# A routed-expert stage of a diffusion backbone: overflow tests nested, block closed without GpSimd's drain, overflow experts on fewer buffers, filter loads issued behind the overflow weights

## The reference

```python
def moe_ffn(xt, rg_w, rg_b, re_w, re_b, w13, w2):
    g_prob = softmax(xt @ rg_w + rg_b)            # 4 groups, the best one is taken
    e_logits = xt @ re_w + re_b                   # 8 experts of that group
    e_w, e_idx = top_k(softmax(e_logits), 2)      # 2 experts per token, weights normalised
    ...
    def expert_block(args):
        xblk, e = args
        gate, up = jnp.split(xblk @ w13[e], 2, axis=-1)
        return (jax.nn.silu(gate) * up) @ w2[e]
    ...
```

## Time and profile before

| | |
|---|---|
| median of 3 runs | 2263.57 us (2260.22 to 2264.07) |
| the profiled execution | 2262.39 us, its span 2260.6 us |
| mean granted clock of TensorE | 0.962 |
| expert stage of layer 0 | about 803 to 1334 us |
| Hyena stage | about 1334 to 1722 us |
| expert stage of layer 1 | about 1723 to 2232 us |
| PE, share of the span busy | 89% |
| bytes moved by DMA | 592.09 MB |

### The profile page before, as it was taken

The page is one execution under the profiler, slowest core; times in us unless marked ns, Lnnn a source line. Parts: engine busy times, 40 slices in busy tenths (PEclk is TensorE's granted clock), DMA queues, the critical chain, the costliest instruction groups (busy, mean ns, idle before and its releaser), DMA issues. The chain is left out here.

```text
span 2260.6 us, 20875 instructions
## 1 busy us (share of the span) xinstructions
PE 2022.6 (89%) x7648; PEld 907.6 (40%) x7648; DVE 789.4 (35%) x1581; ACT 365.9 (16%) x778; POOL 238.0 (11%) x523
## 2 busy tenths in 40 slices
PE   5999999999999969997889859999996999888882
PEld 2555444444443444442333224444554444333330
DVE  3778311235333752221111124464734222111113
ACT  2111212212203121111111112110002111111111
POOL 1000000000000012221222100000000222222120
PEclk9999999999999969999999989999996999999996
DMA  9898522220103589999999961221352999999994
GB/s 363 296 368 318 206 70 87 105 102 34 65 0 114 192 343 423 421 421 422 422 422 423 416 240 59 68 84 35 122 213 99 418 423 420 422 423 422 422 413 162
DMA packets 121191, 592.09 MB, mean 262 GB/s; under 512 B 25704, under 2 KB 43872, under 8 KB 80489
## 3 DMA queue, kind: packets, MB, share of 16 engines
q1 hardware_dynamic: 94494, 548.03, 60.2%
q10 hardware_dynamic: 14412, 25.59, 3.1%
q0 software_dynamic: 12160, 16.83, 2.0%
HBM read 571.13 MB, written 42.31 MB: 271 GB/s over the span
## 5 line engine op out<-in xcount | busy, mean ns | idle before, releaser
L542 PE MATMUL bank<-w,xT 128*64 128x512 f32 x1920 | 433.1, 597 | 45.2 <-DMA w<-in_moe_w 37.3
L562 PE MATMUL bank<-w,hT 128*64 128x512 f32 x1168 | 277.4, 617 | 48.3 <-DMA w<-in_moe_w 40.7
L542 PEld LDWEIGHTS bank<-w,xT 128*64 128x64 f32 x1920 | 154.1, 138 | 310.0 <-issue 258.0
L734 DVE COPY hT<-bank 128x256 f32<-128x256 f32 x73 | 30.9, 424 | 512.9 <-PE bank L550 512.9
L1139 PE MATMUL bank<-uhi,wnh 128*128 128x512 f32 x384 | 168.4, 593 | 0.9 <-ACT uhi L888 0.9
L562 PEld LDWEIGHTS bank<-w,hT 128*64 128x64 f32 x1168 | 89.4, 141 | 185.6 <-issue 138.9
L493 ACT ACTIVATE oh<-bank 128x256 f32<-128x256 f32 x73 | 28.0, 383 | 785.0 <-PE bank L542 785.0
L1535 PE MATMUL bank<-uT,wo 128*128 128x512 f32 x256 | 133.8, 604 | 3.8 <-DVE uT L1421 3.8
L739 DVE TENSOR_TENSOR ohs<-bank,g2h 128x512 f32<-128x512 f32 x73 | 50.5, 691 | 234.6 <-PE bank L562 234.6
L1139 PEld LDWEIGHTS bank<-uhi,wnh 128*128 128x128 f32 x384 | 71.8, 190 | 86.9 <-issue 85.8
L542 PE MATMUL bank<-w13x,xT 128*64 128x512 f32 x416 | 94.4, 593 | 8.0 <-DMA w13x<-in_moe_w 8.0
(11 more groups left out here) (436 smaller groups left out, 2133.1 us busy)
## 6 DMA issues: line engine op xcount, KB each, us to landing
w<-in_moe_w SPq DMA_DIRECT2D x177, 2048.0 KB, 34.7
adab<-in_ada_w SPq DMA_DIRECT2D x24, 2048.0 KB, 11.5
w13x<-in_moe_w SPq DMA_DIRECT2D x18, 2048.0 KB, 34.1
wnh<-in_h_in_w SPq DMA_DIRECT2D x12, 1024.0 KB, 5.2
wo<-in_m_in_w SPq DMA_DIRECT2D x4, 2048.0 KB, 17.9
wo<-in_m_in_w ACTq DMA_DIRECT2D x4, 2048.0 KB, 17.6
ow<-in_m_out_w SPq DMA_DIRECT2D x8, 1024.0 KB, 6.8
d_xm<-xmb ACTq DMA_DIRECT2D x16, 385.5 KB, 5.9
```

What stands on the lines that cost most here:

```text
L542: ins = t_.matmul(b[n * C:(n + 1) * C, :].rearrange("c (g f) -> c g f", g=2), xT[:, k, half * C:(half + 1) * C], w13s[i][:, k, n], start=( ...
L562: ins = t_.matmul(b_y[m * C:(m + 1) * C, :], hT[:, k, half * C:(half + 1) * C], w2[:, u, kk, m * 512:(m + 1) * 512], start=(kk == 0), stop ...
```

## The change

Four edits, all in the expert stage.

1. The 16 overflow bodies no longer stand in 4 groups of 4 behind two levels of tests. Body o stands inside the tests of all bodies before it, so that the first test that fails jumps to the end of all.
2. The block is made with `no_gpsimd_drain=True`, by which GpSimd has no drain at the block's end.
3. The overflow steps use four of the `w13` buffers (1 to 4) and two of the `w2` slots (0 and 1), with new functions for buffer, count and previous user. Buffer 5, buffer 0 and slot 2 are left alone by them. The first overflow step's `w13` halves have buffers 1 and 2 and wait for the same products as before; its `w2` goes to slot 0 instead of slot 2.
4. SP doesn't wait for the overflow body's product2 any more. The loads of `fle` and `dfe` become a function, called where they stood. They wait for the same products as before.

```diff
--- before.py
+++ after.py
@@ -320,7 +320,7 @@
                 w13b = [w13[:, i] for i in RING] + [w13x[:]]
                 w13s = [w.rearrange("p k (g n f) -> p k n g f", g=2, n=2) for w in w13b]
                 y_half = d_y[l].rearrange("s (h d) -> (s h) d", h=2)
-                blk = c.enter_context(nc.Block())
+                blk = c.enter_context(nc.Block(no_gpsimd_drain=True))
 
                 def steps(eng, main, drain, extra):
 
@@ -330,11 +330,10 @@
                             eng.wait_ge(S["meta"], 1)
                             more = eng.value_load(meta[0:1, 0:1], min_val=0, max_val=NOV)
                     drain()
-                    for q in range(0, NOV, 4):
-                        with eng.If(more > q):
-                            for o in range(q, q + 4):
-                                with eng.If(more > o):
-                                    extra(NS + o)
+                    with ExitStack() as taken:
+                        for o in range(NOV):
+                            taken.enter_context(eng.If(more > o))
+                            extra(NS + o)
 
                 def turn(n):
 
@@ -342,7 +341,30 @@
 
                 def half_turn(p, h):
 
+                    if p >= NE:
+                        i = 1 + (2 * (p - NE) + h) % 4
+                        return i, 16 * (len(range(i, 2 * NE, NH)) + (p - NE) // 2 + 1)
                     return (2 * p + h) % NH, 16 * ((2 * p + h) // NH) + 16
+
+                def half_before(p, h):
+
+                    if p >= NE + 2:
+                        return p - 2, h
+                    last = range(half_turn(p, h)[0], 2 * NE, NH)[-1] if p >= NE else 2 * p + h - NH
+                    return last // 2, last % 2
+
+                def down_turn(p):
+
+                    if p >= NE:
+                        u = (p - NE) % 2
+                        return u, 16 * (len(range(u, NE, NB)) + (p - NE) // 2 + 1)
+                    return p % NB, 16 * (p // NB) + 16
+
+                def down_before(p):
+
+                    if p >= NE + 2:
+                        return p - 2
+                    return range(down_turn(p)[0], NE, NB)[-1] if p >= NE else p - NB
 
                 @blk.sync
                 def _(sp):
@@ -362,13 +384,13 @@
                         for h in range(2):
                             i, n = half_turn(p, h)
                             if n > 16:
-                                q, hq = (2 * p + h - NH) // 2, (2 * p + h - NH) % 2
+                                q, hq = half_before(p, h)
                                 sp.wait_ge(S["up" if hq else "upa"], LAST[q] + 1)
                             sp.dma_start(w13b[i], w13v[:, bass.ds(e, 1), h].rearrange("p o k n -> p (o k) n")).then_inc(s_w13l[i], 16)
 
                     def load_second(p, e):
-                        u, _n = turn(p)
-                        sp.wait_ge(S["yp"], LAST[p - NB] + 1)
+                        u, _n = down_turn(p)
+                        sp.wait_ge(S["yp"], LAST[down_before(p)] + 1)
                         sp.dma_start(w2[:, u].rearrange("p (h k) n -> p h k n", h=2), w2v[:, bass.ds(e, 1)].rearrange("p o h k n -> p (o h) k n")).then_inc(s_w2l[u], 16)
 
                     def main(s):
@@ -383,19 +405,21 @@
                         e = expert(1 + P + s - NS)
                         load_first(p, e)
                         load_second(p, e)
-                        sp.wait_ge(S["yp"], s + 1)
 
                     sp.wait_ge(S["meta"], 1)
                     sp.wait_ge(S["vst"], 16 * TL)
+
+                    def load_filters():
+                        if l == 0:
+                            sp.wait_ge(S["yp"], LAST[range(2, NE, NB)[-1]] + 1)
+                            for h in range(2):
+                                sp.dma_start(fle[:, :, h * 512:(h + 1) * 512], d_fl[h]).then_inc(s_fle, 16)
+                            last = range(5, 2 * NE, NH)[-1]
+                            sp.wait_ge(S["up" if last % 2 else "upa"], LAST[last // 2] + 1)
+                            sp.dma_start(dfe[:], I["dft"].rearrange("(t p) f -> p t f", p=P)).then_inc(s_dfe, 16)
+
                     steps(sp, main, lambda: None, extra)
-                    if l == 0:
-                        last = max(p for p in range(NE) if p % NB == 2)
-                        sp.wait_ge(S["yp"], LAST[last] + 1)
-                        for h in range(2):
-                            sp.dma_start(fle[:, :, h * 512:(h + 1) * 512], d_fl[h]).then_inc(s_fle, 16)
-                        last, h = max((i // 2, i % 2) for i in range(2 * NE) if i % NH == 5)
-                        sp.wait_ge(S["up" if h else "upa"], LAST[last] + 1)
-                        sp.dma_start(dfe[:], I["dft"].rearrange("(t p) f -> p t f", p=P)).then_inc(s_dfe, 16)
+                    load_filters()
                     if l == 0:
                         load_route_tables(sp, 1)
 
@@ -551,7 +575,7 @@
                         ins.then_inc(S["hps"], 1)
 
                     def product2(n):
-                        u, loads = turn(ORDER[n - 1])
+                        u, loads = down_turn(ORDER[n - 1])
                         pe.wait_ge(s_w2l[u], loads)
                         pe.wait_ge(S["hT"], n)
                         at_least(pe, S["ya"], n - 1)
```

## The result

| | before | changed |
|---|---|---|
| median of 4 runs | 2261.89 us | 2242.57 us |
| lowest to highest | 2259.92 to 2264.07 | 2240.28 to 2245.6 |
| profiled execution, its span | 2262.39, 2260.6 | 2244.76, 2243.0 |

The ratio is 0.9917, with a 95% interval of 0.9904 to 0.9929.

The account below looks back on a forecast made before the run. Weight transfers on the 16 DMA engines bound the expert stages, so only stage ends could gain. Gains of 3.2 (layer 0) and 2.3 us (layer 1), rounded down to 5.2, from 2263.57 gave 2258.4; range 2250 to 2265.5.

Parts of the forecast that it names:

- it costs 6.2 to 6.36 there: Both expert stage ends: GpSimd's removed block drain moves to L122, serial behind the barrier, costing 6.2 to 6.36 us.
- this case: Both stage ends: the drain is really gone, L122's stays at 0.12; 17.8 us less, 2245.8; chance 0.11.
- Nesting: PE's tests at both stage ends: one price per far jump, 3.6 to 5.1 us; layer 1 arrival 12.3 us earlier.
- Rival 4: PE's tests: one jump over sixteen bodies costs as much as four over four; 9.5 us slower, 2273.1; chance 0.04.
- GpSimd last at both ends: L268, both expert stages: GpSimd arrives last, at 1324.0 us in layer 0 and 2223.4 in layer 1.
- The last scatter's flight: Layer 0's end: with filter loads issued earlier, the last scatter lands 4.1 us after issue instead of 6.5.
- The jump of GpSimd: Layer 0's end: GpSimd's single jump over fifteen overflow bodies after the scatter's landing, taken as 0.5 us.
- rival 3: Layer 0: GpSimd's long jump needs a fetch, 2.8 us, and the scatter gains nothing; 0.8 less, 2262.8; chance 0.18.
- The late w2: Overflow step, layer 0: w2 is issued 15.2 us later but was waiting in line, so cost 0.
- Rival 2: Overflow step, layer 0: the later w2 is exposed and delays product2 by 15.1 us; 9.9 slower, 2273.5; chance 0.05.
- The early loads: SP, layer 0's end: filter and table loads issue from 1295 instead of 1318.46 us; alone worth nothing.
- The sum: Both stage ends: gains of 3.2 us in layer 0 and 2.3 in layer 1, rounded down to 5.2.

Follow-up runs that it names:

- e1: Changed kernel with GpSimd's drain at the expert block's end put back; 2255.41 us, ratio 0.9978.
- e2: Kernel before with only GpSimd's block drain removed; 2260.0 us, ratio 0.9992.
- e9: Changed kernel with a plain GpSimd drain added between the block's barrier and L122's drain at every stage end; 2259.1 us, single execution.
- e10: Changed kernel with a semaphore-resetting drain, then a plain one, ending GpSimd's expert-stage stream; 2244.19 us, single execution.
- e8: Changed kernel with router table loads moved to the Hyena stage and the scatter's index prepared before the wait for the result; 2242.16 us, ratio 0.9919.
- e13: Changed kernel with only the scatter's index preparation moved ahead of its wait for the result; 2243.93 us, ratio 0.9916.
- e6: Changed kernel with SP's wait for the overflow's product2 put back, so filter and table loads issue behind it; 2249.96 us, ratio 0.9951.

## Why the prediction was wrong, step by step

1. **The failed step: "it costs 6.2 to 6.36 there", at L122.** The 6.2 was read rightly as work that a drain starts, and the price is real: e1 puts it back at full length. But "L122's is then the first after the indirect transfers" took the drains as one kind. L122's resets semaphores and does not do that work (e2, e9, e10), and L123's plain one behind it finds nothing. So 6.24 us in layer 0 and 6.07 in layer 1 went away that the forecast had kept: 12.3 of the missing 14.1. The rows at hand did not forbid it: both short drains had only been seen behind the long one, and I gave this case 0.11.
2. **Nesting**: right in its place and size. PE arrives at 2208.6, which is 2218.0 on the time axis of before (9.4 later there), instead of 2231.8 (forecast 2219.5 at the latest), and at 1320.1 in layer 0 (forecast 1319). A far jump is paid once, whatever the distance, but not always with the same price: behind the early loads it is 6.2, above the forecast's bound of 5.1, and PE had time for it. Rival 4 falls.
3. **GpSimd last at both ends**: right; 1324.0 forecast and measured, but the exact agreement is luck. The profiled execution came 1.9 us later to this end, so on the time axis of before it is 1322.1, and 1.5 of the difference is SP's issue stall, which no step had.
4. **The last scatter's flight**: forecast 4.1, measured 4.1. The jump of GpSimd: 0.5 taken, 0.6 measured. In e8 and e13 the jump costs 2.6 and 2.7, the price that rival 3 was given (2.8); that a fetch is behind it is not shown.
5. **The late w2**: cost 0, right; it landed 16.5 us after its issue. Rival 2 falls.
6. **The early loads**: "Alone this is worth nothing, POOL being later" can hold only while the long drain stands inside the block (no run had this edit alone). With that drain out of the block, moved or gone, SP with late loads is the last, and the early ones are worth 4.8 us (e6 against the changed kernel). The sum had this in it without saying so, since it let SP arrive at 1322 at the latest.

With step 1 mended the sum would have been 5.2 + 12.3 = 17.5, and with SP's 1.5 us 19.0, against 19.3 measured. The other 1.7 us by which the forecast was too high lie in its base: 2263.57 from three runs, where four give 2261.89.

## What to carry to other kernels

At a barrier, list every engine's arrival and the next two behind the last: here GpSimd's drain, PE's tests and SP's loads lay over each other, and two edits that alone gave 1.8 and 5.0 us at the two ends gave 14.9 together. Of a step that is removed, ask whether what stands behind it is the same kind of instruction before moving its price there, and give that question the weight that it deserves when the two answers are 12 us apart. When a far jump follows the event that everybody waits for, its stall is on the path (layer 0 of e13, 2.7 us); in front of the event it is free (layer 1).

## What the runs showed of the hardware

- A plain GpSimd drain after indirect transfers takes 0.083 us for each one since the last drain: 6.36 for 77, 6.20 for 75, 2.76 for 33, 2.59 for 31. A second one takes 0.03.
- The drain that resets semaphores (L122) takes 0.06 to 0.13 in the same place, and plain ones behind it 0.04 to 0.05.
- PE's failed test costs 3.3 to 6.6 us when it jumps over four to sixteen bodies and 0.22 to 0.34 over one. Over fifteen it takes 6.17 with SP's loads issued before it and 3.32 with them issued behind it (changed kernel and e6).
- An issue of dfe's load on SP takes 10.26 us behind the overflow's weights and the first filter loads, and 0.61 behind the filter loads alone (changed kernel and e6).
